# Spreading the later groups' front work over the expert fetches by a weight for each kind of piece

## Time and profile before

| what | value |
|---|---|
| median of three runs | 2114.26 us |
| the profiled execution, its own time | 2111.76 us |
| its span, first to last instruction | 2109.9 us |
| mean granted TensorE clock | 0.921 of 2.4 GHz |
| moved by DMA | 755.91 MB, 358 GB/s over the span |
| busy: PE, DVE, ACT, POOL | 79%, 59%, 36%, 29% |
| wait of POOL for the fold that frees a slot | 1037.1 us, 313 times |
| wait of DVE for a fetch | 433.2 us, 315 times |

### The profile page before, as it was taken

The page is one execution under the profiler, slowest core; times in us unless marked ns, Lnnn a source line. Parts: engine busy times, 40 slices in busy tenths (PEclk is TensorE's granted clock), DMA queues, the critical chain, the costliest instruction groups (busy, mean ns, idle before and its releaser), DMA issues.

```text
span 2109.9 us, 25198 instructions
## 1 busy us (share of the span) xinstructions
PE 1656.7 (79%) x8636; PEld 918.5 (44%) x8636; DVE 1237.8 (59%) x3324; ACT 763.7 (36%) x2339; POOL 612.2 (29%) x584
## 2 busy tenths in 40 slices
PE   6999867687777776689989997777777777777776
PEld 4859754453444444356657665442221211211111
DVE  2331289666655368965544446786777775554554
ACT  2120134653533242365463323233333333333332
POOL 0000023423333332222213231225444434333331
PEclk8999987799799987899969998889999999999999
DMA  9683269899899998889948998769999999999996
GB/s 400 243 340 124 100 261 357 360 404 421 326 422 421 421 409 335 355 331 367 396 194 351 420 421 346 230 255 413 421 421 422 421 421 421 422 422 421 421 421 272
DMA packets 107808, 755.91 MB, mean 358 GB/s; under 512 B 14176, under 2 KB 14176, under 8 KB 16416
## 3 DMA queue, kind: packets, MB, share of 16 engines
q0 software_dynamic: 82944, 604.02, 70.0%
q1 hardware_dynamic: 23872, 147.92, 17.6%
q10 hardware_dynamic: 864, 2.36, 0.3%
HBM read 749.52 MB, written 4.73 MB: 357 GB/s over the span
## 4 chain that ended last, share of the span: by engine, by line
DMA 38%; PE 27%; DVE 14%; issue 13%; ACT 5%; POOL 2%; SPq 0%; POOLq 0%; DVEq 0%; ACTq 0%
DMA ring<-in_expert_uv_dram,uidx 35%; PE ps L587 7%; PE ps L847 6%; DVE ring L1506 5%; DMA ring<-in_wpack_dram 3%; PE ps L706 3%; POOL ring L451 2%; PE ps L583 2%; PE ps L712 1%; PE ps L727 1%; PE ps L650 1%; PE ps L617 1%; PE ps L537 1%; PE ps L559 1%; ACT L1098 1%
## 5 line engine op out<-in xcount | busy, mean ns | idle before, releaser
L451 POOL DMA_INDIRECT ring<-in_expert_uv_dram,uidx x576 | 610.9, 1061 | 1416.0 <-PE ps L847 1037.1
L1506 DVE CUSTOM_DVE_ANT_0 ring<-ring,mA 128x1024 f32<-128x1024 f32 x576 | 697.4, 1222 | 436.8 <-DMA ring<-in_expert_uv_dram,uidx 433.2
L847 PE MATMUL ps<-ring,wdiag 128*32 128x512 f32 x2304 | 768.9, 665 | 211.2 <-ACT wdiag L1105 197.3
L847 PEld LDWEIGHTS ps<-ring,wdiag 128*32 128x32 f32 x2304 | 158.8, 118 | 738.6 <-ACT wdiag L1105 441.0
L1098 ACT ACTIVATE gel<-act_in 128x1 f32<-128x1 f32 x576 | 116.5, 202 | 826.7 <-DVE act_in L1506 825.1
L587 PE MATMUL ps<-h,ring 128*128 128x192 f32 (+2 forms) x960 | 174.7, 340 | 29.6 <-DVE work L1229 11.2
L1105 ACT ACTIVATE wdiag<-repeat,wsel 128x32 f32<-128x32 f32 x576 | 185.1, 321 | 18.8
L587 PEld LDWEIGHTS ps<-h,ring 128*128 128x128 f32 x960 | 155.0, 198 | 59.7 <-issue 51.6
L1100 ACT ACTIVATE wsel<-gel,gsel 128x1 f32<-128x1 f32 x576 | 169.7, 295 | 18.7
L767 PE MATMUL ps<-h,ring 128*128 128x192 f32 (+2 forms) x768 | 148.9, 354 | 17.1 <-DVE h L1213 14.7
L767 PEld LDWEIGHTS ps<-h,ring 128*128 128x128 f32 x768 | 131.3, 210 | 40.4 <-issue 22.3
(11 more groups left out here) (205 smaller groups left out, 1511.5 us busy)
## 6 DMA issues: line engine op xcount, KB each, us to landing
ring<-in_wpack_dram SPq DMA_DIRECT2D x132, 1024.0 KB, 12.4
ring<-in_expert_uv_dram,uidx POOLq DMA_INDIRECT x576, 24.6
x<-in_keysT_dram SPq DMA_DIRECT2D x2, 1024.0 KB, 14.9
o_y_p<-mA ACTq DMA_DIRECT2D x16, 128.0 KB, 5.2
bias<-in_bias_dram SPq DMA_DIRECT2D x1, 1024.0 KB, 28.8
o_v_p<-kv SPq DMA_DIRECT2D x4, 256.0 KB, 11.6
o_k_p<-x SPq DMA_DIRECT2D x4, 256.0 KB, 5.3
x<-in_x_c_dram SPq DMA_DIRECT2D x1, 1024.0 KB, 7.7
```

The source lines that it names most:

```text
L451: nc.gpsimd.indirect_dma_start(out=ring[:, slot, :], out_offset=None, in_=ins["expert_uv"], in_offset=bass.IndirectOffsetOnAxis(ap=uidx[:, ...
L847: mm = nc.tensor.matmul(pY[c * GT:(c + 1) * GT, half, :], wdiag[:, n % NDIAG, :], ring[:, ROW[n][0], D + half * 512:D + (half + 1) * 512], ...
L1506: nc.vector.tensor_tensor_reduce(r, r, h2n[:, g % 2, :], 1.0, 0.0, ALU.mult, ALU.add, act_in[:, g % 2, j:j + 1]).then_inc(s["dot"], 1)
```

## The change

`spread()` no longer hands out the pieces evenly by their number, but by a weight for each kind, and its work for group 1 and the place of set 1 and 2 come earlier.

```diff
 PLACE_AT = [None] + [GT * FIRST[p] - AHEAD for p in range(1, 5)]
+PLACE_AT[1] -= AHEAD
+PLACE_AT[2] -= 8
 RUN = REP * (PH - 1)
...
+def effort(g, tick):
+
+    kind, x, y = tick
+    product = 4 * max(0.38, 0.0018 * N[g])
+    if kind == "norm":
+        return 4.0
+    if kind == "at":
+        return 1.5
+    if kind == "rt" and y == 0 and x:
+        return 7.0
+    if kind == "z" and y == 1 and ZR[g][x][0] in ("qk", "X"):
+        return 1.4 if g == 1 else 2.0
+    return product / 2.0 + (0.2 if kind == "mg" and y >= 4 else 0.0)
+
+
+COST = [[effort(g, t) for t in TICKS[g]] for g in range(3)]
+
+
 def spread(out, g, n, start, end):
 
     done = sum(e[0] == g and len(e) == 2 and isinstance(e[1], tuple) for e in out)
-    left = TICKS[g]
-    while done < len(left) and done * (end - start) < (n + 1 - start) * len(left):
-        out.append((g, left[done]))
+    while done < len(TICKS[g]) and sum(COST[g][:done]) * (end - start) < (n + 1 - start) * sum(COST[g]):
+        out.append((g, TICKS[g][done]))
         done += 1
```

## The result

The changed kernel takes 2135.62 us (median of 4 runs, 2132.98 to 2138.27) against 2114.52 us for the kernel before on the same chip: a ratio of 1.0099, 95% interval 1.0082 to 1.0117, some 21 us slower. The profiled execution took 2136.98 us with a span of 2135.2 us, 25.3 us longer than before's.

What follows compares the result with a forecast made beforehand. Bounds vary by stage: DMA in group 1's columns, merge and output projection, DVE in its retrieval, PE in group 2's columns and merge. Group 1 -15 and group 2 +21 gave +6 us: 2118 profiled, 2120 median, range 2090 to 2145.

Steps and rivals of the forecast that it cites:

- my own case: Whole kernel: the summed stage changes give 2120 us as the median, own range 2105 to 2135, chance 0.47.
- 2.49 us per fetch where DMA binds: Group 1's other columns, merge and output projection: fewer fetches save 2.49 us each, -22.4, -42.3 and -17.4.
- the merge where PE is full: Group 2's merge: 34 to 25 fetches, PE stays full, so only -9.5 us.
- the empty stretches: Fetches without pieces behind them: +25 us up to fetch 172, -15 for old 172 to 180, +7.5 after 297.
- group 2's retrieval: 24 to 38 fetches; stepped head by head, 164 us against 130, +34.
- group 1: Fetches up to 172: savings in columns, merge and output projection against longer retrieval and empty stretch, -15 us together.
- Second norm: +4 x 1.2: Group 1's second norm: four more fetches at DVE's price of a dot, +4.8 us.
- the retrieval: +36: Group 1's retrieval: 30 to 46 fetches, stepped head by head, 157 us against 121.
- A: Both retrievals: heads overlap, PE folding while DVE searches, -46 us, 2074; 2097 if half; chance 0.27 whole or half.
- B: Late retrieval heads: PE's waiting brings the 1.2 GHz clock for products behind it, +25 + 10, 2155 us; chance 0.11.
- C: Group 2's merge and columns give nothing, weight blocks come late in group 1's merge: +12 + 9.5, 2141 us; chance 0.10.
- D: Whole kernel: order hardly matters because DMA evens it out, 2114 us; chance 0.05.

Runs made afterwards that it cites:

- two kernels that differ by one fetch: Changed kernel with group 2's retrieval heads fixed at four fetches each: from 263 + 4x 2118.49 us, from 262 + 4x 2177.24 us.
- the weights of group 1 alone: Changed kernel with piece weights kept for group 1 only, group 2 evenly spread from 172 to 300: 2112.98 us, ratio 0.9941 to the kernel before.
- products first: Changed kernel with each retrieval head's weight moved from first piece to last, so all 16 products stand right behind the scores: 2104.68 us, ratio 0.9902.
- the moves: Changed kernel with every weight set to 1, keeping the moved places and group 1's earlier end: 2114.92 us, ratio 0.995 to the kernel before.
- the kernel with group 2 sooner: Kernel before with one line, PLACE_AT[2] -= 8: group 2 starts at fetch 172, group 1's front ends at 164; 2114.3 us, ratio 0.9952.
- the last step: Group 2's norms weighted 2.5 and heads 4.6 instead of 4.0, against the kernel with group 1's heads at 9.0: 2081.88 us, ratio 0.9804 to before.
- the kernel with the fold third: Changed kernel with group 2's four-fetch heads at 262 + 4x, last three pieces behind the third fetch: 2177.24 us, ratio 1.0251.
- the one with the fold second: Changed kernel with group 2's four-fetch heads at 263 + 4x, last three pieces behind the third fetch: 2118.49 us, ratio 0.9977.

## Why the prediction was right, and where its sizes were off

**The sign and the mechanism were right.** I had given slower 0.51, with 2120 us and 2090 to 2145; the time is 2135.6, within that range and half a us outside what I had called my own case (2105 to 2135). The forecast was +6 us where +21 came. Many steps held one by one (table above): 2.49 us per fetch where DMA binds (-42.3, measured -41.7; -22.4, measured -21.6), the merge where PE is full (-9.5, measured -7.3), the empty stretches (+25, measured +26.4), and group 2's retrieval (+34, measured +35.8). Group 2 as a whole (+21, measured +22) agrees in part by luck: columns, attention and output projection gave back 11.7 us more than forecast, where five fetches of the columns were worth 1.7 us each and not 0.5, and norms and q/k columns took 7.4 more. That a fold third or fourth in a head makes the long interval (stepped 21 to 22 us, measured 22 to 24) and the fold second the short one (17, measured 16.6 and 17.4) came as stepped, and two kernels that differ by one fetch confirm it.

**What was mis-sized is group 1**: -15 forecast, +3 measured, which is 18 of the 19 us between the forecast and the profiled execution. Two terms hold it. The experiments agree: the weights of group 1 alone moved the time by -2 us.

First, "Second norm: +4 x 1.2". The stage took 13.3 us more for the four fetches, which is DMA's price of 2.49 and more. I had priced the dots by DVE, because the norm leaves DVE waiting for other engines. But the stages ahead of it run at the DMA's pace, so no fetched rows are in store when the norm comes. Between 674 and 704 us DVE waits five times for a fetch, 9.4 us in all. Two of these waits, 4.7 us, end in the stage itself or at its end. The wait for PE's part of the norm is 5.0 us, where it was 1.45 before: 3.5 us more. With four dots at 1.15 us, 4.6, these make 12.8 of the 13.3 us. The dots are what I had; the waits are what I had left out.

Second, the retrieval: +36, measured +45.7. The seven intervals sum to 150.6 us, where I had 139. All seven took longer than stepped; heads 3 to 5 took 23.6, 22.6 and 22.6 where I had 20.5, 18.3 and 20.5. What I had left out is the tile's own work, which in heads 3 and 4 meets the same late fold (timeline of the changed kernel in group 1, in the head whose search began at 768.2):

```profile
779.49 3.62 PE L866 MATMUL ps<-ring,wdiag 128*32 128x512 f32 x4 [8.67 <-ACT wdiag L1124]
...
782.90 3.11 PE L885 MATMUL ps<-ident,x 128*32 128x128 f32 x16
...
786.05 1.23 DVE L1541 TENSOR_TENSOR mA<-mA,ps 32x1024 f32<-32x1024 f32 x1 [4.09 <-PE ps L885]
```

Once in each tile of 32 fetches, DVE scales and adds the sums, and in its stream these stand between the dots. PE's part of it (L885 here, L876 in the head before) is queued behind the late fold, so DVE stops for 4.1 and 4.9 us in the middle of its dots. The fold and PE's part run slower than elsewhere (3.62 and 3.11 us, where as many instructions of each took 1.90 us in the head before and 1.94 us in group 2). I had put 3.4 us for the lower clock over all seven heads. Head 5 has no such work in it; why it took 2.1 us more than stepped is open.

**The rivals.** A (the heads overlap, 2074 to 2097) did not come with this change, but the runs show that its price was right: with the products ahead of the fetches the time falls by 42 us, where I had put -46 for the whole of A. The condition that I had named, products done before the last dot of the head, is the one that the edit brings about. The rule of the Trainium skill ("Perfetto Trace Analysis", Optimization Strategy) that interleaving regimes may improve performance is not borne out by the change alone. With the products first it is in group 1 (483.8 us against 503.8), where the fetches come out of stages that the DMA holds. In group 2, where PE holds them, it is not: 541.5 us against 529.0. B (the clock, 2155) is a part of what happened, some 30% of a late head (2.2 of 7.5 us), not a case of its own. C's weight blocks did come late in group 1's merge, on two lines of PE (groups by line, 551 to 645 us):

```profile
L725 PE MATMUL ps<-h,ring 128*128 128x128 f32 x256 | 35.5, 302 | 7.9 <-DMA ring<-in_wpack_dram 6.8 <-DVE work L1352 1.1
L731 PE MATMUL ps<-work,ring 128*128 128x128 f32 x128 | 19.0, 309 | 10.8 <-DMA ring<-in_wpack_dram 10.4 <-ACT work L1036 0.4
```

That is 17 us, where rows 6 had 6 in the other group, and more than the 12 that I had as the upper bound. No cost of it is seen: the stage was held by the DMA itself at 408 GB/s and came out at 94.6 us against 94 forecast, which is what its 26 fetches and 12 blocks take at 2.49 us each. C's number, 2141, lies nearer to the measured time than my 2120, but neither of its causes came: group 2's merge and columns gave 15.6 us back. D (no difference) is excluded.

**What stays open.** Where the 10 us lie that the moves win: the kernel before was profiled on the first chip alone, and there its fetch 308 is at 1424.2 us, as in the kernel with group 2 sooner on a slower chip (1424.6). What in the last step won 10 us was read from stages only. Whether folds issued two fetches later would serve as well as products first was not tried.

## What to carry to other kernels

When a stage is widened by filler work, price the filler by what binds that stage, and then look at what the filler is put in front of in each in-order stream: here 42 us hung on whether the products of a head stood before or behind its five or six fetches, and 59 us on one fetch of offset. Taking filler out of a stage that another engine holds anyway gives back little (7 us for nine fetches in group 2's merge, 42 for seventeen in group 1's), and then the filler does not pay even in a good order: group 2 stayed 12 us behind its even spread with products first. An interval stepped from a single odd case in the old trace (19.08 us among 14s) foretold the new intervals within 4.3 us each, most of them too short.

## What the runs showed of the hardware

The one behaviour with a price was TensorE's clock: in the stretch that follows 8.4 us without work it is granted at 0.50, the 1.2 GHz level, and the fold of one fetch takes 3.62 us, where it takes 1.90 after a wait of 1.93 us. After a wait of 3.1 us both are seen: 3.62 us in the kernel with the fold third (at 1266.08), 1.90 in the one with the fold second (at 1263.66). A fold of one fetch, at full clock, takes as long as one of four (1.90 and 1.94 us). And chips differ: the same kernel took 2114.5 us on one and 2123 to 2125 us on three others, half of this change's effect, so runs on different chips are compared by their ratios alone.
